# Transformer layer with top-4-of-32 experts, one core: the expert products with unsplit fp32 weights over four column parts of 32, one part at a time

## What is computed

```python
def moe(h, w_router, b_router, w_gu, b_gu, w_down, b_down):
    logits = (ht @ w_router + b_router)
    top_v, top_i = lax.top_k(logits, TOP_K)
    gate = jax.nn.softmax(top_v, axis=-1)
    ...
    def expert_block(args):
        xb, e = args
        gu = xb @ w_gu[e] + b_gu[e]
        g = jnp.minimum(gu[:, :D_EXPERT], SWIGLU_LIMIT)
        lin = jnp.clip(gu[:, D_EXPERT:], -SWIGLU_LIMIT, SWIGLU_LIMIT)
        act = g * jax.nn.sigmoid(SWIGLU_ALPHA * g) * (lin + 1.0)
        return act @ w_down[e] + b_down[e]
    ...
```

## Time and profile before

| what | us |
|---|---|
| median of 2 runs | 1587.34 (1587.03 to 1587.64) |
| profiled execution, first to last instruction | 1587.7 |
| TensorE busy in it | 1561.6 |
| DVE busy | 1278.0 |
| ACT busy | 1079.0 |
| POOL busy | 475.5 |

### The profile page before, as it was taken

How to read it: one execution, slowest core, us unless ns; L and a number is a source line. 1 busy time by engine, 2 the same in 40 slices (tenths; PEclk the granted TensorE clock), 3 DMA queues, 4 the chain that set the end, 5 groups by cost and what they waited for, 6 DMA issues and landing times.

```text
span 1587.7 us, 22175 instructions
## 1 busy us (share of the span) xinstructions
PE 1561.6 (98%) x7662; PEld 1132.1 (71%) x7662; DVE 1278.0 (80%) x1022; ACT 1079.0 (68%) x967; POOL 475.5 (30%) x252
## 2 busy tenths in 40 slices
PE   8999999999999999999999999999999999999997
PEld 7866688888866677767776676677676766766764
DVE  3768724327699998999999899999998999999884
ACT  5468723224468777877777778777777877777773
POOL 0000210000022943333444333344443333444420
PEclk9999999999899999999999999999999999999999
DMA  7310022436399999999999999999999999999984
GB/s 268 117 60 21 8 90 74 139 120 270 125 364 351 363 373 371 390 368 377 371 370 373 371 377 376 372 376 368 365 375 372 367 381 372 371 377 360 383 317 136
DMA packets 103174, 467.50 MB, mean 294 GB/s; under 512 B 13641, under 2 KB 14177, under 8 KB 70337
## 3 DMA queue, kind: packets, MB, share of 16 engines
q1 hardware_dynamic: 94928, 449.23, 73.8%
q0 software_dynamic: 7872, 17.68, 5.1%
q10 hardware_dynamic: 336, 0.08, 0.0%
HBM read 456.82 MB, written 19.79 MB: 300 GB/s over the span
## 4 chain that ended last, share of the span: by engine, by line
PE 91%; DVE 7%; issue 1%; DMA 0%; ACT 0%; DVEq 0%; POOL 0%; ACTq 0%; POOLq 0%
PE ps L1801 28%; PE ps L1819 14%; PE ps L1804 14%; PE ps L1824 7%; PE ps L1463 6%; PE ps L1465 6%; PE ps L1464 6%; PE ps L1490 4%; DVE l_w L1195 3%; PE ps L1616 1%; DVE head_max L1124 1%; PE ps L1791 1%; PE ps L1572 1%; DVE probs L1142 1%; PE ps L1734 0%
## 5 line engine op out<-in xcount | busy, mean ns | idle before, releaser
L1195 DVE TENSOR_TENSOR l_w<-a_w,h_w 128x2048 fp32r<-128x2048 f32 x384 | 865.8, 2289 | 35.3 <-ACT h_w L841 32.6
L841 ACT ACTIVATE h_w<-a_w 128x2048 fp32r<-128x2048 f32 x384 | 731.1, 1915 | 230.3 <-PE ps L1804 165.0
L977 POOL TENSOR_TENSOR mark_sb<-ones 1x1 f32<-1x1 f32 x93 | 267.4, 2876 | 642.3 <-ACT y_sb L886 632.3
L1801 PE MATMUL ps<-h_w,xt_hi 128*96 128x512 f32 x1024 | 282.8, 397 | 0.5 <-ACT xt_hi L864 0.5
L1801 PE MATMUL ps<-h_w,xt_lo 128*96 128x512 f32 x1024 | 278.8, 394 | 1.0 <-DVE xt_lo L1349 1.0
L1804 PE MATMUL ps<-l_w,xt_hi 128*96 128x512 f32 x1024 | 278.6, 393 | 0.5 <-DVE l_w L1195 0.5
L1801 PEld LDWEIGHTS ps<-h_w,xt_lo 128*96 128x96 f32 x1024 | 165.6, 162 | 73.0 <-DVE xt_lo L1349 1.8
L1804 PEld LDWEIGHTS ps<-l_w,xt_hi 128*96 128x96 f32 x1024 | 165.6, 162 | 72.3 <-DVE l_w L1195 1.0
L1801 PEld LDWEIGHTS ps<-h_w,xt_hi 128*96 128x96 f32 x1024 | 160.4, 162 | 71.1 <-issue 7.6
L1819 PE MATMUL ps<-h_w,at_hi 128*96 128x512 f32 x512 | 162.1, 398 | 0.2 <-issue 0.2
L1819 PE MATMUL ps<-h_w,at_lo 128*96 128x512 f32 x512 | 159.5, 392 | 0.0
(11 more groups left out here) (260 smaller groups left out, 1566.7 us busy)
## 6 DMA issues: line engine op xcount, KB each, us to landing
a_w<-in_w_gate_up SPq DMA_DIRECT2D x256, 1024.0 KB, 8.4
a_w<-in_w_down SPq DMA_DIRECT2D x128, 1024.0 KB, 7.9
w_raw<-in_w_in SPq DMA_DIRECT2D x8, 2048.0 KB, 7.8
w_raw<-in_w_out SPq DMA_DIRECT2D x2, 2048.0 KB, 7.7
w_raw<-in_w_in SPq DMA_DIRECT2D x2, 1024.0 KB, 7.6
x_sb<-in_x SPq DMA_DIRECT2D x8, 256.0 KB, 7.3
w_raw<-in_w_mem_kv SPq DMA_DIRECT2D x1, 2048.0 KB, 10.9
x<-in_x SPq DMA_DIRECT2D x4, 512.0 KB, 5.1
```

The costliest lines, as they stand in the source:

```text
L841: nc.scalar.activation(h_w[m % H_SLOTS][:], a_w[m % A_SLOTS][:], ACT.Copy).then_inc(wh_done, 1)
L977: nc.gpsimd.tensor_tensor(mark_sb[:], ones[0:1, 0:1], ones[0:1, 0:1], ALU.mult).then_inc(marked, 1)
L1195: nc.vector.tensor_tensor(l_w[m % A_SLOTS][:], a_w[m % A_SLOTS][:], h_w[m % H_SLOTS][:].bitcast(F32), ALU.subtract).then_inc(wl_done, 1)
L1801: nc.tensor.matmul(ps[0:SLOTS, n, :], x_part[:, k, :], w_h[:, n * COLS:(n + 1) * COLS], start=False, stop=False)
```

## The change

The weights are no longer split. The raw fp32 tiles go straight to TensorE as the moving operand, and so do tokens and activations as the stationary one. `moe_high`, `moe_low`, `low_xt` and `low_act` are gone, with `h_w` and `l_w`; the room goes to 16 gate-up tiles `gu_w` (two jobs) and 4 down tiles `dn_w`.

TensorE's 128 columns are used as four parts of 32. Part q holds 32 token slots and writes PSUM partitions 32q to 32q+31; it computes the weight columns of quarter q. The 96 slots are three groups g of 32, each in a PSUM bank of its own. So a gate-up tile has 4 x 3 matmuls (two times 256 moving columns, 512 in all, 32 stationary columns), and a down tile 2 x 4 x 3 of 256 columns:

```diff
-                for k in range(KD):
-                    m = m0 + k
-                    w_h, w_l = h_w[m % H_SLOTS], l_w[m % A_SLOTS]
-                    wait_high(pe, i, m)
-                    for x_part in (xt_hi, xt_lo):
...
-                        for n in range(4):
-                            nc.tensor.matmul(ps[0:SLOTS, n, :], x_part[:, k, :], w_h[:, n * COLS:(n + 1) * COLS], start=False, stop=False)
-                    wait_low(pe, i, m)
-                    for n in range(4):
-                        last = nc.tensor.matmul(ps[0:SLOTS, n, :], xt_hi[:, k, :], w_l[:, n * COLS:(n + 1) * COLS], start=False, stop=k == KD - 1)
+                    w = gu_w[s * KD + k]
+                    pe.wait_ge(gu_in[s * KD + k], loads * 16)
+                    for q in range(4):
+                        for g in range(TRIOS):
+                            last = nc.tensor.matmul(ps[quarter(q), g, :], xt[:, k, quarter(g)],
+                                                    w[:].rearrange("p (h n) -> p h n", h=2)[:, :, q * QCOLS:(q + 1) * QCOLS],
+                                                    start=False, stop=k == KD - 1, skip_group_check=True)
                     last.then_inc(gemm_ps, 1)
...
+                for c in range(DN_PARTS):
+                    pe.wait_ge(dn_in[c], j * 16 + 16)
+                    for h in range(2):
+                        for q in range(4):
+                            for g in range(TRIOS):
+                                last = nc.tensor.matmul(ps[quarter(q), 3 + g, 0:QCOLS], act_t[:, TRIOS * h + g, quarter(c)],
+                                                        dn_w[c][:, h * D + q * QCOLS:h * D + (q + 1) * QCOLS],
+                                                        start=c == 0 and h == 0, stop=c == DN_PARTS - 1 and h == 1, skip_group_check=True)
```

```diff
             def add_rows(s):
-                nc.gpsimd.indirect_dma_start(out=x_rows, out_offset=bass.IndirectOffsetOnAxis(ap=sum_row[:, s:s + 1], axis=0),
...
+                for g in range(TRIOS):
+                    nc.gpsimd.indirect_dma_start(out=x_rows.rearrange("r (q n) -> (r q) n", q=4),
+                                                 out_offset=bass.IndirectOffsetOnAxis(ap=sum_row[:, s, g:g + 1], axis=0),
...
```

More of the change, by code:

```diff
@@ L38 @@
 SLOTS = 96
+QUARTER = 32
+TRIOS = SLOTS // QUARTER
+QCOLS = D // 4
 MAX_JOBS = (SEQ * TOP_K + N_EXP * (SLOTS - 1)) // SLOTS + 1
@@ L325, in encoder_kernel @@
         first_in = sem("first_in")
-        part_in = [sem(f"part_in{i}") for i in range(12)]
+        gu_in = [sem(f"gu_in{i}") for i in range(16)]
+        dn_in = [sem(f"dn_in{i}") for i in range(4)]
+        bias_of_in = sem("bias_of_in")
+        bias_of_ready = sem("bias_of_ready")
         x2_in = sem("x2_in")
@@ L621, in _ @@
             for k in (6, 7):
-                load_gu(0, k, k)
+                load_gu(0, 0, k)
+            for q in (0, 1):
+                load_dn(0, q)
             for t in range(TB):
@@ L1388, in _ @@
-            step.link(nc.vector.tensor_tensor(sg_sb[:], sg_sb[:], y_sb[:], ALU.mult))
-            dve.wait_ge(l_ready, 1)
-            nc.vector.scalar_tensor_tensor(out=act_sb[:], in0=act_sb[:], scalar=1.0, in1=sg_sb[:],
-                                           op0=ALU.add, op1=ALU.mult).then_inc(act_ready, 1)
-            for m in range(LOW_LEAD + 4, LOW_LEAD + KD):
-                moe_low(0, m)
+            activate(0)
+            take_sum_rows()
             pairs_but_one = dve.value_load(job_table[0:1, 1, 1:2], min_val=MIN_PAIRS - 1, max_val=NJ // 2 - 1)
@@ new lines, in turn_act, with spread_slots @@
+                for k in range(2 * TRIOS):
+                    last = turn(6 + k // TRIOS, (k % TRIOS) * P, act_sb[:, k, :])
+                last.then_inc(at_ps, 1)
+            def spread_slots():
+                pe.wait_ge(slot_table_ready, 1)
+                pe.wait_ge(same_slot_ready, 1)
+                for g in range(TRIOS):
+                    last = nc.tensor.matmul(ps[:, 3, g * 2 * NJ:(g + 1) * 2 * NJ], same_slot[:, g, :], slot_table[:].rearrange("p v j -> p (v j)"),
+                                            start=True, stop=True, skip_group_check=True)
+                last.then_inc(sum_ps, 1)
@@ new lines, in quarter, with gate_up @@
+            def quarter(q):
+                return slice(QUARTER * q, QUARTER * (q + 1))
+            def gate_up(j, s, loads, between):
+                pe.wait_ge(bias_row_in[s], loads * (16 * TRIOS))
+                for g in range(TRIOS):
+                    rows = slice(QUARTER * g, QUARTER * g + 8)
+                    nc.tensor.matmul(ps[:, g, :], bias_of[rows, :], bias_row[s][rows, :].bitcast(F32R), start=True, stop=False,
+                                     skip_group_check=True)
+                pe.wait_ge(xt_done, j + 1)
+                for k in range(KD):
+                    w = gu_w[s * KD + k]
+                    pe.wait_ge(gu_in[s * KD + k], loads * 16)
+                    for q in range(4):
+                        for g in range(TRIOS):
+                            last = nc.tensor.matmul(ps[quarter(q), g, :], xt[:, k, quarter(g)],
+                                                    w[:].rearrange("p (h n) -> p h n", h=2)[:, :, q * QCOLS:(q + 1) * QCOLS],
+                                                    start=False, stop=k == KD - 1, skip_group_check=True)
@@ L1823, in down, with down_last @@
+            def down_last(j):
+                pe.wait_ge(y_ready, j + 1)
+                pe.wait_ge(act_t_done, j + 1)
+                for c in range(DN_PARTS):
+                    pe.wait_ge(dn_in[c], j * 16 + 16)
+                    for h in range(2):
                         for n in range(2):
-                            last = nc.tensor.matmul(ps[0:SLOTS, 4 + n, :], at_hi[:, 2 * q + k, :], w_l[:, (2 * k + n) * COLS:(2 * k + n + 1) * COLS],
-                                                    start=False, stop=q == DN_PARTS - 1 and k == 1)
+                            for g in range(TRIOS):
+                                last = nc.tensor.matmul(ps[quarter(g), 4 + n, :], act_t[:, TRIOS * h + g, quarter(c)],
+                                                        dn_w[c][:, h * D + n * COLS:h * D + (n + 1) * COLS],
+                                                        start=c == 0 and h == 0, stop=c == DN_PARTS - 1 and h == 1, skip_group_check=True)
@@ L1826, in down @@
                     last.then_inc(gemm_ps, 1)
-                    between(q)
             pe.wait_ge(xg_in[0], 16)
```

384 lines of the change are left out of this document (158 added, 226 removed).

## The result

The changed kernel takes 2059.24 us (median of 2 runs, 2059.09 to 2059.4) against 1587.34: a ratio of 1.296 (95% interval 1.294 to 1.299). The forecast was 1537. The profiled execution spans 2057.2 us, 469.5 more than before.

The account below looks back on a forecast made before the run. The prediction took the expert stage as PE-bound. Thirty-one jobs at 33.5 instead of 35.17 us (-52), first gate-up -1.6, last down product +2.7, row-additions +2 and start -1 gave -50: 1537.5 us, own range 1505 to 1600, 8-in-10 range 1505 to 2550.

Parts of the forecast that it names:

- I take n = 6: Weight tiles in gate-up and down: all four column parts compute at once, a tile takes 6 instruction times; job 33.5 us.
- rival (B): Gate-up and down: two or three waiting instructions per part; job 64.4 or 43.8 us, total 2510 or 1860 us; chance 0.20.
- h: Number of instructions that may wait in one column part while TensorE goes on to the next; at least 1.
- a lag of parts behind one another after each change of shape ... I take nothing: Last column part starting behind the first, six times a job: at most 1.2 us each, +220 us; counted as nothing.
- The forecast's own case: Expert stage with four parts at once and no new bound: job 33.5 us instead of 35.17, total 1537.5 us; chance 0.56.
- 8 x 6 x 0.43: First gate-up alone: eight tiles of 6 instruction times at 0.43 us, 20.6 us against 22.2, so -1.6.
- rival (E): Expert stage: DMA binds at 372 GB/s (1590 us) or four parts pay 7% (1604 us), no measurable gain; chance 0.05.
- The price of 0.14 us for each of six changes of shape: Between differently shaped TensorE instructions: 0.14 us per change, six a job; bounds nothing and 0.3 us.
- I price the DMA at nothing: Weight loads: 393 GB/s needed in a 33.5 us job, 426 seen, so no cost; bound: job stays at 35 us.
- The last down product +2.7: End of the expert stage: 8 groups of 12 instructions over three parts, 13.8 us against 11.1.
- -1: Start of the expert stage: PE's idling for the removed splitting work goes, worth 1 us.
- Rival (D): Gate-up and down: matmuls keep program order, a tile takes 20 instruction times; job 105.7 us, total about 3820 us; chance 0.08.

Follow-up runs that it names:

- the in-turn kernel with the early biases: Against the changed kernel: gate-up and down calls alternate over the column parts, and SP issues final gain and down biases before the last four down tiles; 1546.09 us.

## Why the prediction was wrong

**The failing step is "I take n = 6".** The measured 2059 lies within the 8-in-10 range, which was stretched to 2550 for rival (B), but not within the forecast's own, 1505 to 1600, and the kernel is slower where it was forecast to be faster. The step rests on h of 4 or more, and h is 3, so n is 8, the lower case of rival (B). The trace of before shows a part overtaking one waiting instruction, and the text said itself that it doesn't show whether the limit is 1 or 15. What tipped the choice was weak on both counts. "A rule needs no small limit" is a thought about design and no row. And the four weight loads between 103.60 and 103.73, taken as "nothing was held back", come from a program in which a part never has more than one waiting. They can't bear on a limit above that. The model around the number was right: parts overtake each other, the next part starts 5 - h instruction times later, and n = 4 x (5 - h) gives 8 with h = 3. The runs of 4, 6 and 12 instructions confirm the count.

**The size within rival (B)** was too low: 43.8 us a job and 1860, measured 49.25 and 2059. Three terms were mis-sized. First, "a lag of parts behind one another after each change of shape ... I take nothing". The lag is real, though not from the engine's speed of issue: it is the same hold-up, 4 instruction times at each start of the stream, twice 1.78 us for the gate-up and 0.92 for the down product, 4.5 in a job. The bound of 1.2 us at each start was for another cause, and too small for a start of the gate-up. Second, with three parts out of step the spacing is 0.445 and 0.231 instead of 0.43 and 0.215, 2 us in a job. Third, what stands between came to 2.04 instead of 2.5. And 43.8 + 4.5 + 2 - 0.5 is 49.8; the half microsecond over lies where the first down tile runs into the last gate-up tile: 1063.02 - 1036.75 is 26.27 us, and 52 x 0.445 + 16 x 0.231 would be 26.84.

**The forecast's own case was well priced.** In turn a job takes 33.42 (predicted 33.5). So "8 x 6 x 0.43", the rate of four parts with no loss between them, and the 2.5 us of transposes, bias and shape changes hold as sums. The 7% of rival (E) isn't paid. The price of 0.14 us for each of six changes of shape is only a mean. Moving the activations' turn behind the bias takes two of the six out of a job, the one from the bias to the gate-up and the one from the gate-up to the transposes, and it saved 0.13 us in turn and not 0.28. The first of the two costs next to nothing (0.43 us from the start of the bias to the gate-up, where the bias was priced 0.41), the second 0.13 (5.29 us for 12 x 0.43 = 5.16).

**"I price the DMA at nothing"** was right for the changed kernel, where SP waits 1226 us for PE. For the forecast's own 33.5 us a job it would have come out nearly right by luck: the loads sustain 34.25, and the lead with which they start covered the difference in 26 of the 30 jobs of the in-turn kernel with the early biases; three near the end paid 3.4 us. The 426 GB/s of one stretch of 10 us isn't a rate that lasts: with PE starved the loads stay at 382 to 395 in the stretches of 100 us from 500 to 1400. (35.17 us x 372 GB/s in 33.5 us is 391 GB/s; the text has 393.) The lower end of the range, 1505 with free shape changes, was out of reach: the kernel that gives TensorE only about 18 us of work in a job takes 1531.

**Tail and start.** "The last down product +2.7": 8 groups of 12 at three parts were to be 13.8 us, and 16.39 were measured at a mean clock of 0.85 in that stretch; 13.8 / 0.85 is 16.2. So the price was right for the full clock and the clock was not foreseen. The wait of 9.38 us for `down_bias` was in no term, as I had not followed SP's queue behind the last down tiles. At the start +6.1 instead of -1: PE idles 5.79 us before the first bias group, put down to issue, and 3 to 6 us in all the later kernels. What it waits for was not tested.

The Trainium skill, page "TensorE: Matmul & The Clock Gate", Part 3, "The mechanism", has matmuls keep program order in start and end. Rival (D), worked out under that, would have been 3820 us, and four parts would never have run together in runs of four. The measurements decide otherwise: part 3's first instruction starts ahead of nine waiting ones. The window of 64 instructions that the same section gives isn't what limits matmuls here: in the runs of six and of twelve the engine stops at one running and three waiting.

## What to carry to other kernels

When TensorE's columns are split into parts, issue the parts in turn. In these runs, with parts of 32 columns, a part holds one running and three waiting instructions; with more of it in a row the engine stops for all parts. With four parts a round of R instructions each took 4 x (R - 4) instruction times instead of R, 8 for 6 and 32 for 12. An unsplit fp32 call counts as two, so three such calls in a row are already too many and two are not. A busy share near 100% hides this; count how many instructions run in a stretch shorter than one. A mean over all jobs hides a lead that is being used up and a slow first job; list the jobs one by one. And where a row shows a mechanism only at its smallest size, take the limit as unknown, and look for an order that doesn't depend on it: here it was an exchange of two loops.

## What the runs showed of the hardware that I had not expected

- The hold-up is per part and counts instructions: three waiting in each of three parts, nine in all, are let pass, and a fourth in one part stops everything (runs of 4, 6 and 12: 1559, 2059 and 2919 us, the last with its long runs in the gate-up alone).
- Once the parts are staggered, they stay so to the next instruction over the whole array, and a step of three parts takes 0.445 us instead of 0.43. Why was not tested.
- A lasting stream of weight loads moves 382 to 395 GB/s in stretches of 100 us, some 8% under the best stretch of 10 us (426), and needs 34.25 us for a job's weights with PE starved for them.
- After PE's pause of 9.4 us near the end the granted clock stood at 0.50 and 0.52 for ten us, and eight small matmuls took 3.78 instead of 1.99 us. After a pause of only 2 us at the same place, in the kernel with the early biases and the two with half of the down loads, it was 0.82, 0.50 and 0.66 from 1510 to 1515.
